# Adaptive-modulation products on GpSimd instead of VectorE, with their weight slots spread evenly through the stream, in a fused two-block transformer kernel

## The reference, cut to what matters

```python
def ada_modulation(c, w, b):
    mod = jax.nn.silu(c) @ w + b
    return jnp.split(mod[:, None, :], 6, axis=-1)

def even_layer(x, c, ...):
    sh_m, sc_m, g_m, sh_f, sc_f, g_f = ada_modulation(c, ada_w, ada_b)
    h = rms_norm(x, norm_mix) * (1 + sc_m) + sh_m
    ...
    x = x + g_m * mix
    h = rms_norm(x, norm_ffn) * (1 + sc_f) + sh_f
    return x + g_f * swiglu(h, ffn_gate, ffn_up, ffn_down)
```

## Time and profile before

| | |
|---|---|
| median of 3 runs | 1715.72 us |
| lowest, highest | 1714.87, 1740.07 us |
| profiled execution | 1743.0 us, span 1741.0 us |
| mean granted TensorE clock in it | 0.909 |
| busy: PE, PEld, DVE, ACT, POOL | 92%, 76%, 71%, 52%, 0% |
| HBM read | 356 MB, 205 GB/s over the span |

### The profile page before, as it was taken

One profiled execution on the slowest core, in us unless ns is written; L12 is line 12 of the kernel. 1 busy time (PEld: TensorE's weight loads), 2 busy tenths in 40 slices (PEclk: granted clock), 3 DMA queues, 4 the chain that ended last, 5 costly groups with the idle time before them and its releaser, 6 DMA issues.

```text
span 1741.0 us, 20071 instructions
## 1 busy us (share of the span) xinstructions
PE 1597.5 (92%) x7386; PEld 1316.0 (76%) x7387; DVE 1242.2 (71%) x1681; ACT 899.8 (52%) x1123; POOL 4.3 (0%) x16
## 2 busy tenths in 40 slices
PE   5899999988999999789899998969879999999995
PEld 4778877776878878678788887858767887788874
DVE  4757888655457887664678875684478888888887
ACT  4545553434346653444443334432357777777774
POOL 0000000000000000000000000000000000000000
PEclk9999999996699999895899999865789999999998
DMA  7544447663044448460267675310248888897882
GB/s 309 218 168 146 182 181 292 239 241 122 24 175 164 166 171 315 151 229 34 97 250 279 256 263 192 145 49 1 73 147 325 319 307 318 299 342 302 308 316 116
DMA packets 54264, 358.17 MB, mean 206 GB/s; under 512 B 7088, under 2 KB 8112, under 8 KB 13360
## 3 DMA queue, kind: packets, MB, share of 16 engines
q1 hardware_dynamic: 51392, 353.47, 54.6%
q0 software_dynamic: 144, 2.10, 0.3%
q10 hardware_dynamic: 2656, 1.64, 0.3%
HBM read 356.13 MB, written 1.05 MB: 205 GB/s over the span
## 4 chain that ended last, share of the span: by engine, by line
PE 74%; DVE 15%; ACT 5%; issue 5%; DMA 1%; PEldq 0%; DVEq 0%; PEld 0%; ACTq 0%; SPq 0%
PE ps L413 19%; PE ps L415 19%; PE ps L414 19%; DVE wlo L1293 5%; PE ps L572 4%; PE ps L592 3%; PE ps L581 2%; PE ps L775 2%; ACT whi L918 2%; PE ps L524 1%; DVE tok L1421 1%; DMA head_scratch<-w_s_dram 1%; DVE tok L1832 1%; PE ps L548 1%; ACT ps L930 1%
## 5 line engine op out<-in xcount | busy, mean ns | idle before, releaser
L1293 DVE TENSOR_TENSOR wlo<-raw,whi 128x2048 fp32r<-128x2048 f32 (+1 forms) x303 | 651.1, 2171 | 186.4 <-ACT whi L918 174.5
L918 ACT ACTIVATE whi<-raw 128x2048 fp32r<-128x2048 f32 (+1 forms) x303 | 546.8, 1822 | 294.2 <-PE ps L415 293.9
L413 PE MATMUL ps<-whi,xhi 128*128 128x512 f32 (+3 forms) x1360 | 537.5, 395 | 22.9 <-DVE xlo L1366 8.0
L415 PE MATMUL ps<-whi,xlo 128*128 128x512 f32 (+3 forms) x1360 | 526.4, 387 | 0.0
L414 PE MATMUL ps<-wlo,xhi 128*128 128x512 f32 (+3 forms) x1360 | 526.0, 387 | 0.0
L413 PEld LDWEIGHTS ps<-whi,xhi 128*128 128x128 f32 x1360 | 260.2, 191 | 80.0 <-DVE wlo L1293 12.0
L415 PEld LDWEIGHTS ps<-whi,xlo 128*128 128x128 f32 x1360 | 259.6, 191 | 52.4
L414 PEld LDWEIGHTS ps<-wlo,xhi 128*128 128x128 f32 x1360 | 260.7, 192 | 48.2
L413 PE MATMUL ps<-whi,ahi 128*128 128x512 f32 x440 | 178.3, 405 | 12.8 <-DVE wlo L1293 12.8
L414 PE MATMUL ps<-wlo,ahi 128*128 128x512 f32 x440 | 174.9, 398 | 0.0
L415 PE MATMUL ps<-whi,alo 128*128 128x512 f32 x440 | 174.8, 397 | 0.0
(11 more groups left out here) (230 smaller groups left out, 1265.9 us busy)
## 6 DMA issues: line engine op xcount, KB each, us to landing
raw<-stream_dram SPq DMA_DIRECT2D x318, 1024.0 KB, 5.2
raw<-stream_dram SPq DMA_DIRECT2D x30, 512.0 KB, 4.1
attn_scratch<-toep_dram POOLq DMA_DIRECT2D x1, 2048.0 KB, 7.9
raw<-stream_dram SPq DMA_DIRECT2D x2, 528.0 KB, 5.7
h<-x_dram SPq DMA_DIRECT2D x1, 1024.0 KB, 5.5
y<-tok SPq DMA_DIRECT2D x2, 512.0 KB, 2.7
head_scratch<-w_s_dram ACTq DMA_DIRECT2D x1, 512.0 KB, 18.5
gates<-fg_dram ACTq DMA_DIRECT2D x1, 512.0 KB, 21.7
```

What stands on the lines that cost most here:

```text
L413: pe.matmul(o, xh, wh, start=start, stop=False)
L415: return pe.matmul(o, xl, wh, start=False, stop=stop)
L918: act.activation(whi[:, q % SPL, 0:w], raw[:, s % RAW, 0:w], ACT.Copy).then_inc(sem("hi_done"), 1)
L1293: dve.tensor_tensor(wlo[:, q % SPL, 0:w], raw[:, s % RAW, 0:w], whi[:, q % SPL, 0:w].bitcast(F32), ALU.subtract).then_inc(sem("lo_done"), 1)
```

## The change

GpSimd takes over `modulate`. In the slot's own buffer it multiplies the four 128x512 blocks by their columns of `cs` (silu(c)), adds blocks 2 and 3 to blocks 0 and 1 in one 128x1024 add, and adds the two that are left into `acc`: one add for an even slot, two for an odd one. It waits for `ada_cols` of the chunk before (TensorE has read `acc`) ahead of its first write to `acc`, and raises `ada_added` at a slot's end. SP's load that reuses a modulation slot's buffer waits for `ada_added`; `lo_done` counts weight slots alone.

The slots' places change: slot number m, from 0, follows weight slot 5 + int(2.75 m) - 1 (q 4, 6, 9, 12, 15, ...), through all stages up to q 133, up0 and up1 among them (before: every second weight slot in the other stages, up to q 143). TensorE's turn of a chunk comes three weight slots behind its odd slot (`turn_after`: q 9, 15, 20, 26, 31, 37, 42, 48, 53, 59, 64, 70, 75, 81, 86, ...), and VectorE's `ada_cols` four weight slots behind that, in `split`. The bias DMA stands in GpSimd's list ahead of the 17th modulation slot. The host code writes the stream in the new order; sizes and values are the same.

```diff
@@ -93,6 +93,7 @@
 
 
 ADA = 24
+FIRST_ADA, ADA_STEP, ADA_LAG = 5, 2.75, 3
 
 
 class Plan:
@@ -102,47 +103,47 @@
     def __init__(self):
         self.width, self.kind, self.q, self.at, self.qat, self.ada = [], [], [], {}, {}, []
         self.nq = 0
-        left = [ADA, ADA]
-
-        def add(widths, layer=None, first=0):
-            for i, w in enumerate(widths):
+        self.ada_after = []
+
+        def add(widths):
+            for w in widths:
                 self.kind.append("w")
                 self.width.append(w)
                 self.q.append(self.nq)
                 self.nq += 1
-                if layer is not None and i >= first and i % 2 and left[layer]:
-                    n = ADA - left[layer]
-                    left[layer] -= 1
+                if len(self.ada) < 2 * ADA and self.nq == FIRST_ADA + int(len(self.ada) * ADA_STEP):
+                    self.ada_after.append(self.nq - 1)
                     self.kind.append("a")
                     self.width.append(SLOT)
-                    self.q.append(None)
-                    self.ada.append((len(self.kind) - 1, layer, n))
+                    self.q.append(len(self.ada))
+                    self.ada.append((len(self.kind) - 1, *divmod(len(self.ada), ADA)))
 
         def begin(name):
             self.at[name], self.qat[name] = len(self.kind), self.nq
 
-        def proj(name, n, order=None, kt=KT, layer=None, first=0):
+        def proj(name, n, order=None, kt=KT):
             begin(name)
-            add([k * w for _, w in chunks_of(n, order) for k in slots_of(kt, w)], layer, first)
+            add([k * w for _, w in chunks_of(n, order) for k in slots_of(kt, w)])
 
         def expert():
             add([SLOT] * 10 + [SLOT // 2] * 2 + [SLOT] * 5 + [SLOT // 2])
 
-        proj("gmlp_in", 2 * D, G_ORDER, layer=0, first=4)
-        proj("gmlp_out", D, layer=0)
+        proj("gmlp_in", 2 * D, G_ORDER)
+        proj("gmlp_out", D)
         proj("up0", 2 * FF)
-        proj("down0", D, kt=FK, layer=0)
+        proj("down0", D, kt=FK)
...
@@ -153,7 +154,8 @@
         begin("more")
         expert()
         begin("end")
-        self.s_of = [s for s, q in enumerate(self.q) if q is not None]
+        self.s_of = [s for s, k in enumerate(self.kind) if k == "w"]
+        self.turn_after = {self.ada_after[2 * g + 1] + ADA_LAG: g for g in range(ADA)}
 
 
 class Tally:
@@ -325,7 +327,7 @@
 
         def wait_lo(eng, q, i=None, per=0):
 
-            eng.wait_ge(sem("lo_done"), PL.s_of[q] + 1 if i is None else i * per + (PL.s_of[q] + 1))
+            eng.wait_ge(sem("lo_done"), q + 1 if i is None else i * per + (q + 1))
 
 
         @block.sync
@@ -333,8 +335,11 @@
             sp.dma_start(h[:, :, :], x_in.rearrange("o (t p) d -> p (o t) d", p=P)).then_inc(sem("x_landed"), 16)
             sp.dma_start(cols[:, :], cols_in).then_inc(sem("cols_landed"), 16)
             def load(s, i=None, src=None):
-                if s >= RAW:
-                    sp.wait_ge(sem("lo_done"), s - RAW + 1 if i is None else i * EXP + (s - RAW + 1))
+                if s >= RAW and PL.kind[s - RAW] == "a":
+                    sp.wait_ge(sem("ada_added"), PL.q[s - RAW] + 1)
+                elif s >= RAW:
+                    done = PL.q[s - RAW] + 1
+                    sp.wait_ge(sem("lo_done"), done if i is None else i * EXP + done)
                 w = PL.width[s]
                 src = s if src is None else src
                 at = stream_in[src, :, 0:w] if i is None else stream_in[bass.ds(i * EXP + src, 1), :, 0:w].rearrange("o p n -> p (o n)")
@@ -396,11 +401,39 @@
                             pattern=[[1, P]], channel_multiplier=-1).then_inc(sem("consts"), 1)
 
 
-            g.wait_ge(sem("h_added"), 4)
-            g.dma_start(bias, toep_in).then_inc(sem("toep_landed"), 16)
-            g.wait_ge(sem("toep_landed"), 16)
-
-            g.memset(bias[0:DH, :, P + DH:S], NEG).then_inc(sem("bias_ready"), 1)
+            added = [0]
+
+            def link(ins):
+                added[0] += 1
+                ins.then_inc(sem("mod"), 1)
+                g.wait_ge(sem("mod"), added[0])
+
+            def modulate(s, layer, n):
+
+                chunk = layer * (ADA // 2) + n // 2
+                g.wait_ge(sem(f"landed{s % RAW}"), 16 * (s // RAW + 1))
+                w = raw[:, s % RAW, :].rearrange("p (k c) -> p k c", k=4)
+                for k in range(4):
+                    kk = 4 * (n % 2) + k
+                    m = g.tensor_scalar(w[:, k], w[:, k], cs[:, kk:kk + 1], None, ALU.mult)
+                link(m)
+                link(g.tensor_tensor(w[:, 0:2], w[:, 0:2], w[:, 2:4], ALU.add))
+                if n % 2 == 0:
+                    if chunk:
+                        g.wait_ge(sem("ada_cols"), chunk)
+                    g.tensor_tensor(acc[:, :], w[:, 0], w[:, 1], ALU.add).then_inc(sem("ada_added"), 1)
+                else:
+                    link(g.tensor_tensor(acc[:, :], acc[:, :], w[:, 0], ALU.add))
+                    g.tensor_tensor(acc[:, :], acc[:, :], w[:, 1], ALU.add).then_inc(sem("ada_added"), 1)
+
+            g.wait_ge(sem("cs"), 1)
+            for s, layer, n in PL.ada:
+                if PL.ada_after[layer * ADA + n] >= QAT["kv"] + 2 and PL.ada_after[layer * ADA + n - 1] < QAT["kv"] + 2:
+                    g.wait_ge(sem("h_added"), 4)
+                    g.dma_start(bias, toep_in).then_inc(sem("toep_landed"), 16)
+                    g.wait_ge(sem("toep_landed"), 16)
+                    g.memset(bias[0:DH, :, P + DH:S], NEG).then_inc(sem("bias_ready"), 1)
+                modulate(s, layer, n)
 
 
         @block.tensor
@@ -442,7 +475,8 @@
                         if mid is not None and j == 0 and t == 0:
                             mid()
                     last.then_inc(sem("w_used"), 1)
-                    ada_turn(PL.s_of[q] + 1)
+                    if q in PL.turn_after:
+                        ada_turn(PL.turn_after[q])
                     if after is not None:
                         after(j)
                     k0 += n
@@ -535,19 +569,14 @@
                         transposes(n_tr)
                 down(FK, lambda: transposes(n_tr))
 
-            turned = [0]
-
-            def ada_turn(s):
-
-                if (s, turned[0] // (ADA // 2), 2 * (turned[0] % (ADA // 2)) + 1) not in PL.ada:
-                    return
-                if turned[0]:
-                    pe.wait_ge(sem("ada_taken"), turned[0])
-                pe.wait_ge(sem("lo_done"), s + 1)
+            def ada_turn(g):
+
+                if g:
+                    pe.wait_ge(sem("ada_taken"), g)
+                pe.wait_ge(sem("ada_added"), 2 * g + 2)
                 for j in range(4):
                     m = pe.matmul(ps[:, 4, j:j + 1], acc[:, j * P:(j + 1) * P], ones[:, 0:1], start=True, stop=True)
                 m.then_inc(sem("ada_cols"), 1)
-                turned[0] += 1
 
             def broadcast_gates():
 
@@ -1292,34 +1320,8 @@
                     dve.wait_ge(sem("hi_done"), q + 1 if i is None else i * per + (q + 1))
                     dve.tensor_tensor(wlo[:, q % SPL, 0:w], raw[:, s % RAW, 0:w], whi[:, q % SPL, 0:w].bitcast(F32),
                                       ALU.subtract).then_inc(sem("lo_done"), 1)
-                    if s + 1 < len(PL.kind) and PL.kind[s + 1] == "a":
-                        modulate(s + 1)
-
-            def modulate(s):
-
-                _, layer, n = PL.ada[seen[0]]
-                assert PL.ada[seen[0]][0] == s
-                seen[0] += 1
-                g = layer * (ADA // 2) + n // 2
-                if n % 2 == 0:
-                    if g == 0:
-                        dve.wait_ge(sem("cs"), 1)
-                    elif n:
-                        ada_cols(g - 1)
-                dve.wait_ge(sem(f"landed{s % RAW}"), 16 * (s // RAW + 1))
-                for k in range(4):
-                    kk = 4 * (n % 2) + k
-                    wk = raw[:, s % RAW, k * W:(k + 1) * W]
-                    if kk == 0:
-                        m = dve.tensor_scalar(acc[:, :], wk, cs[:, 0:1], None, ALU.mult)
-                    else:
-                        m = dve.scalar_tensor_tensor(acc[:, :], wk, cs[:, kk:kk + 1], acc[:, :], ALU.mult, ALU.add)
-                    if k < 3 or n % 2 == 0:
-                        link(m)
-                    if k == 3 and n % 2 == 0:
-                        dve.sem_inc(sem("lo_done"), 1)
-                if n % 2:
-                    m.then_inc(sem("lo_done"), 1)
+                    if q - 4 in PL.turn_after:
+                        ada_cols(PL.turn_after[q - 4])
 
             def ada_cols(g):
```

25 lines of the change are left out of this document (12 added, 13 removed).

## The result

The changed kernel took 1780.8 us (median of 4 runs, 1776.5 to 1785.2), the kernel before beside it 1727.9 (1714.9 to 1743.5): ratio 1.033, 95% interval 1.022 to 1.044. It is slower, by more than I forecast. To read these numbers one thing is needed: in the second attention (at the end of stage e_in) the kernel before runs either at the lower TensorE clock or at the higher one, and takes 1740 to 1744 or 1714 to 1716 us; the changed kernel was profiled with the lower, and its four runs have mean clocks (0.905 to 0.907) that belong to the lower.

What follows compares the result with a forecast made beforehand. TensorE, busy 92% of the span, bounds the kernel, so only its gaps can yield gains. Gains -14.0, turns +4.0, blocking +24 and +5, clock +4 sum to +23 on 1715.7: 1739 us, range 1700 to 1765.

Steps and rivals of the forecast that it cites:

- The base: Whole kernel: a difference worked out on the profiled execution of 1743 us (span 1741) was put on the median, 1715.7 us.
- Gains, -14: VectorE's modulation taken away: q projection 5.0, e_in 4.2, gMLP 1.5, clock at q and e_in 3.3; sum 14.0 us.
- Turns, +4: Five of 24 turns of tiny matmuls had cost nothing at stage ends; moved, each costs 0.81 us: 4.0 us lost.
- GpSimd's durations: GpSimd's modulation slots: tensor_scalar 0.7 us, adds 1.1 and 2.1; a pair of slots 13.1 us, upper end 18.7.
- sign of being wrong: GpSimd's slots taking over 12 us each, or up0 lengthening with no overlap of GpSimd, would show the forecast wrong.
- rival D: Raw ring runs dry because GpSimd's slots, stretched by waiting for VectorE, pass 6 us to spare; 1750 to 1790 us; chance 0.03.
- Blocking, +24 in the loops and +5 outside: VectorE's SBUF-only instructions wait for GpSimd's: eight turns in up0 and up1 at 3.0 us, elsewhere three casts at 1.5.
- The sign for it: In up0 and up1, TensorE's L413 waits for `wlo` eight or so times by 2 to 3 us.
- Clock, +4: TensorE's new stalls of 2 to 3 us sometimes bring its clock down: 4 us.
- B: No interference between VectorE and GpSimd: only gains and turns count, -10 us, 1706 us; chance 0.26.
- C: Strong blocking of VectorE by GpSimd: slower, from +34 us on, 1774 with all 59 us of blocking; chance 0.21.
- The point from which it decides: Strong blocking, +34 us, is reached when a turn in the FFN loops costs 4.4 us instead of 3.0.

Runs made afterwards that it cites:

- without the products: The kernel before with VectorE's modulation products left out, places and turns as before: 1729.4 us, lower clock throughout.
- places alone: The changed kernel with GpSimd's products and adds left out; places, loads, turns and longer hold stay: median 1708.6 us at the higher clock, 1732 at the lower.

## Why the prediction was wrong

I forecast 1739 us, +23 on 1715.7; measured were 1781, and +40 at the same clock. Blocking of VectorE by GpSimd was the right mechanism. Three steps of the sum failed: the base on which I put the difference (25 us off), the clock that the new stalls take along (4 us forecast, some 19 in the profiles), and the casts outside the two loops (5 forecast, 17 measured).

**The base.** "I work out a difference and put it on the median": this step alone is 25 us off. The profile that I read was of the 1741 kind, the median of three of the 1714 kind. I saw the spread from 1714.9 to 1740.1 and took it for noise; the 0.50 of the granted clock over 51 us of the second attention stood in that profile. With the change, none of the runs had the higher clock there. On 1741 my sum gives 1764.

**Gains, -14.** The sum was right, -12 without the products, but part of that is luck. Ahead of the q projection, where I had 5.0, only 2.7 of the 5.45 us went at the old places (at the new ones nearly all: kv 54.2 to 49.0 us and q 90.3 to 87.7 with places alone). gMLP's gap went from 2.35 to 0.97 us, near the 1.5 forecast, but its two stages became 4.9 us shorter together, and the down projections and their normalisations 3, for which I had nothing. And they are gains of a kernel without GpSimd work: with it, the gap ahead of q kept 4.08 of 5.45 us, since I took the products away and did not put the blocking in their place.

**Turns, +4.** Right in sum (3 for places and turns together). The eight turns in up0 and up1 cost 6.4 us there (133.0 and 133.3 against 130.1 and 129.8), 0.8 each as forecast, and elsewhere half of that came back.

**GpSimd's durations.** Wrong for the products: 1.56 us undisturbed (the least of 192), outside my bounds of 0.54 to 0.89, which I had scaled from a memset and an affine_select; a multiply by a column is neither. The adds were near: 2.40 and 1.29 us for 2.1 and 1.1. A pair takes 21.2 us undisturbed instead of 13.1, above my upper end of 18.7, and with its waiting 27 (649 us for 24 pairs). A slot of 13.5 us is over the 12 that I had named as a sign of being wrong, and I had not thought of GpSimd waiting for VectorE except in rival D. The ring still held: ScalarE's `whi` waited for a load once (5.7 us), and TensorE did not stop behind it, so rival D did not occur.

**Blocking, +24 in the loops and +5 outside.** The mechanism stood up: two-input instructions hold VectorE off, the four instructions without slack pass it on, and TensorE waits for `wlo`. The size, from the windows over up0 and up1: TensorE idle for 10.3 and 9.1 us of them, with places alone for none. That is 19.4 / 8 = 2.4 us a turn for the 3.0 forecast. The sign for it came out as forecast: eight stops of 1.0 to 3.9 us in the two loops. That the size is near is luck, from errors of opposite sign: the products, which I let block like the rest, hardly do, and the adds do so for longer. Outside the loops I had counted three casts, 5 us; idle time there rose by 36.2 - 19.4 = 17 us, in nearly every stage as far as e_out, 3.8 of it ahead of the q projection alone. My reading, beyond that one place: with GpSimd busy for 37% of the span, and most of it ahead of stage e_down, any cast without slack meets it.

**Clock, +4.** The worst of the sum. Against places alone, TensorE's busy time rose by 43.5 us with the same matmuls, 24.6 of them in e_in (the second attention) and 19 elsewhere, 12.5 in the two loops. The mean granted clock fits: 0.905 for 0.928 is, as an estimate, 94 us more at half the clock, which cost 47. Behind stops of 1.9 to 3.9 us, as the one shown above, the clock falls to 0.50, three times in up0 alone. So the change's 55 us between these two profiles, the second attention aside, are 36 of idle time and 19 of clock, where I had 29 and 4. (In the medians it is 49 and not 55: the profiled execution of the changed kernel was the slowest of its four, that of places alone 3 us under its median.)

**The rivals.** B (no interference, 0.26) is out. C (from +34 on) is what happened, and I gave it 0.21; even its upper end, 1774 us, lies below the 1781 measured, as it stood on the wrong base. The point from which it decides, 4.4 us a turn, was nearly met (up0 and up1 are 17.6 and 14.4 us longer than with places alone: 32.0 / 8 = 4.0 with the clock), and losses outside the loops did the rest.

## What to carry to other kernels

Before work is moved to GpSimd, ask not how long it takes there but how many tensor operands in SBUF each instruction reads: here 390 us of tensor_scalar cost 8 us, and 184 us of two-input instructions 42. A GpSimd that makes only the products by tensor_scalar, with the adds somewhere else, follows from this and was not tried as a whole kernel. Price a stall of TensorE with the clock that it takes along, and look for stretches in which TensorE is busy for 100% at half the clock: a stop at their entry may be all that keeps them there. Where a few runs differ by more than they scatter, find out by the granted clock which kind the profile is before a difference is put on a median.

## What the hardware showed that I had not expected

- A GpSimd tensor_scalar of 128x512 takes 1.56 us, a two-input add of 512 columns 1.29, of 1024 2.40, and a two-input product of 2048 with a spread column 3.60: the product with two tensor inputs does four blocks in less time than three by tensor_scalar.
- GpSimd waits for VectorE too: the slowest tensor_scalar took 5.7 us for its own 1.56; it ran beside the rest of one `wlo` and the whole of the next.
- Three attentions ran at half the clock for 184 us in sum, with TensorE busy without a break, and at the full clock with the same work once the stops at their entries were filled, in the end 1.3 us in one and 4.0 of 4.7 in another. Matmuls that compute nothing bought 4.6%, 3% against the best run of before. Why this takes so little stays open, and so does why the second attention came out both ways with equal entries: with places alone it stayed at 1.00 with stops of 0.72 and 0.78 us at its entry, more in sum than the 1.3 us that brought the first one down.
